# Matmuls that read the un-normalized stream, and interleaved MLP groups, in a two-layer decoder step

## The chip, the cores and the metric

The kernel runs on one core of one Trainium2 chip. The metric is the device time of one execution in microseconds (us).

## What is computed

One inference step of a decoder with two layers over 256 prompt tokens and 8 x 8 sample tokens, 320 tokens in all, each a row of 1024 float32 numbers. Layer 0 mixes with an mLSTM (a matrix memory), layer 1 with block-sparse attention over a paged cache of 64 pages; each layer has an MLP of width 4096 behind it. Around them stands a residual with a LayerNorm after it:

```python
def layer_norm(x, g, b):
    mu = x.mean(-1, keepdims=True)
    var = jnp.square(x - mu).mean(-1, keepdims=True)
    return (x - mu) * lax.rsqrt(var + LN_EPS) * g + b
...
for layer in range(DEPTH):
    h = mlstm_mixer(...) if layer < N_A_LAYERS else attend(q, ctx) @ w_out_b
    x = layer_norm(ALPHA * x + h, ln_g[layer, 0], ln_b[layer, 0])
    x = layer_norm(ALPHA * x + jnp.square(relu(x @ w_up)) @ w_down, ln_g[layer, 1], ln_b[layer, 1])
```

Between the layers `kv = x @ w_kv` gives the keys and values of the second layer, and `q = x @ w_q` its queries. There are four norms: l = 0 behind the mLSTM, 1 behind its MLP, 2 behind the attention, 3 behind the last MLP.

## The kernel before

**Layout.** The stream X lies turned: 128 partitions of model width by 8 chunks by 320 tokens. So a norm's mean is a sum over partitions and chunks, and its mean, variance and rstd are tiles of 128 x 320 with equal rows.

**Dense tiles.** All weights together are 24 quads of 8 tiles, 192 tiles. A tile is 1024 inputs by 128 outputs. Precision is bought with two rounded float32r halves: `split` in ScalarE rounds a weight tile to its high half (L893), `split` in VectorE subtracts for the low half (L1215), and `dense` (L454) multiplies, chunk by chunk, high by high, high by low, low by high: 24 matmuls of 320 columns. There are four buffers of each half, and four of raw weights, each of two tiles, which SyncE loads as they come free. The result of tile t goes to bank t % 2; the tile after next waits until it is read (`evac` counts that). `dense3` (L469) runs three tiles side by side behind a norm, in more banks, chunk by chunk as the norm's chunks come.

**Order.** The quads are the mLSTM's q/k, v and output gate, its output projection Q_WOA, eight for MLP 0, keys, values, queries (Q_WK, Q_WV, Q_WQ), the attention's output projection Q_WOB and eight for MLP 1. Each engine's program is written out in its own order, with semaphores between them. In an MLP a loop of four rounds runs one up quad (1024 of the 4096 hidden units) and its down quad. Of an up tile ScalarE reads the bank with relu (L1037), VectorE squares (L1449), ScalarE rounds to `HH` (L1040), VectorE subtracts to `HL` (L1451). Of a down tile VectorE adds the bank to X (`residual`, L1363 and L1365).

**A norm.** GpSimd sums x and x squared over chunks 0 to 6 (`sums`, L1641 to L1648), TensorE sums over partitions with a matrix of ones (`ln_stats`, L652 to L657), VectorE forms mean and variance (L1399 to L1403), ScalarE takes logarithm and exponential for a first rstd (L1003, L1004), VectorE centres chunks 0 to 3 (L1406) and GpSimd chunks 4 to 7 (L1655), VectorE refines rstd by a Newton step (L1409 to L1411), then multiplies by rstd and applies gain and bias (L1424, L1434, L1419; ScalarE L1012 for some chunks). Only then come the two halves `XH` and `XL` for the next matmuls (L1008, L1018, L1428, L1415). GpSimd afterwards multiplies X by ALPHA (L1662) for the next residual.

**Around the first norm.** During Q_WOA VectorE also updates the sample state (L1386), and GpSimd has prepared the masked values (L1674) while the last output-gate tiles ran. Behind norm 0 `prompt_state` (L636) runs on TensorE, and ScalarE copies and stores its results (L1046 to L1053).

Of the kernel before, what the change touches and what calls it, by code (L numbers as in the profile page):

```python
# [38 lines left out]
SIDE_BY_SIDE = (Q_MLP0, Q_WK, Q_MLP1)  # L39
UPS = [Q_MLP0 + 2 * g for g in range(4)] + [Q_MLP1 + 2 * g for g in range(4)]  # L40
ACT_QUADS = sorted([Q_QK, Q_V, Q_O, Q_WK, Q_WV, Q_WQ] + UPS)
NT = 8 * N_QUADS
RAW, SPL = 4, 4
# [73 lines left out]
def evac(t):  # L117

    q = t // 8
    mine = q in ACT_QUADS  # L120
    before = sum(1 for x in range(q) if (x in ACT_QUADS) == mine)
    return (0 if mine else 1), 8 * before + t % 8 + 1


def build(nc, x_prompt, x_sample, state_C, state_n, state_m, cache_k, cache_v, page_table,
# [4 lines left out]
    with ctx:  # L130
# [21 lines left out]
        HH = put("h_hi", [128, NC8, T], F32R)  # L152
        HL = put("h_lo", [128, NC8, T], F32R)
# [12 lines left out]
        lnT = put("ln_cols", [128, 64])  # L166
        bg = put("b_gate", [40, 1])
# [25 lines left out]
        npr_at = [a[0]]  # L193
# [3 lines left out]
        vm_at, az_at, cq_at = [xh_at], [hh_at], [fs_at]  # L197
# [28 lines left out]
        ln_at = [vreg]  # L226
        mu = put("ln_mu", [128, T], F32, ln_at)
        var = put("ln_var", [128, T], F32, ln_at)
        rs = put("ln_rstd", [128, T], F32, ln_at)
        tmp = put("ln_tmp", [128, T], F32, ln_at)  # L230
        assert ln_at[0] <= b_[0]
# [10 lines left out]
        ko_at, yo_at = [b_[0] - 8192], [b_[0] - 16384]  # L242
# [14 lines left out]
        def sem(name):  # L257
# [4 lines left out]
        s_ev = [sem("act_emptied"), sem("dve_emptied")]  # L262
        s_x = sem("x_in")
# [46 lines left out]
        def dense_bank(t):  # L310


            if t % 8 == 4 and t // 8 in (Q_MLP0, Q_MLP1):
                return ps[5]
            return ps[9 - t % 8] if t % 8 in (2, 3) and t // 8 in SIDE_BY_SIDE else ps[t % 2]

# [19 lines left out]
        def wsrc(u):  # L336

            q, j = u // 4, u % 4
            c = 256 * j
            w, c0 = {Q_QK: (win, 0), Q_V: (win, 1024), Q_O: (win, 2048), Q_WOA: (w_out_a[0], 0),  # L340
                     Q_WK: (w_kv, 0), Q_WV: (w_kv, 1024), Q_WQ: (w_q_b[0], 0), Q_WOB: (w_out_b[0], 0)}[q]
            return lhs_k(w[:, c0 + c:c0 + c + 256])
# [11 lines left out]
        def _(sp):  # L354
            def load_unit(u, src, more=0):
                if isinstance(more, int) and u < RAW:
                    pass
                else:
                    sp.wait_ge(s_lo, 2 * (u - RAW) + 2 + 2 * more)
                sp.dma_start(raw[u % RAW][:, :, :], src).then_inc(s_raw[u % RAW], 16)  # L360
# [5 lines left out]
            load_unit(0, wsrc(0))  # L366
            load_unit(1, wsrc(1))
# [5 lines left out]
            load_unit(2, wsrc(2))  # L373
            load_unit(3, wsrc(3))
# [8 lines left out]
            for u in range(4, 16):  # L383
                load_unit(u, wsrc(u))

            def mlp_loads(first, m):
                with sp.Fori(0, 4) as g:
                    for j in range(4):
                        load_unit(4 * first + j, lhs_k(w_up[m][:, bass.ds(g * 1024 + 256 * j, 256)]), 8 * g)
                    for j in range(4):  # L390
                        load_unit(4 * first + 4 + j,
                                  lhs_k(w_down[m][bass.ds(g * 1024, 1024), 256 * j:256 * j + 256]), 8 * g)

# [1329 lines left out]
```

## Time and profile before

| | us |
|---|---|
| median of 3 runs | 1020.72 |
| lowest, highest | 1020.37, 1023.13 |
| span of the profiled execution | 1020.9 |
| TensorE busy in it | 950.1 |
| VectorE | 566.2 |
| ScalarE | 402.2 |
| GpSimd | 130.4 |
| TensorE, its mean granted clock | 0.964 |

The profile is one execution. Busy shares are averages over stages, so the place to look is the timeline around each norm and the windows of TensorE, not the total. In the rows further down PE is TensorE, PEld its weight loads, DVE VectorE, ACT ScalarE, POOL GpSimd, SPq or ACTq the DMA issues of SyncE or ScalarE; brackets give the idle time before an instruction and who ended it. The granted clock is 1.00 at 2.4 GHz and 0.50 at 1.2 GHz.

### The profile page before, as it was taken

Reading aid. Unit: us, or ns where it says so; the run is one execution under the profiler, and the core shown is the slowest. Engines: PE = TensorE matmul, PEld = TensorE weight load, DVE = VectorE, ACT = ScalarE, POOL = GpSimd, SP = SyncE. Lnnn points to the kernel's source line nnn. Section 1 sums busy time; section 2 is a strip of 40 time slices with the busy share of each in tenths; the row PEclk is TensorE's granted clock in tenths of the full one; section 3 lists DMA queues with packets and bytes.
Section 4 is the critical chain, followed back from the end, with each engine's and each line's share of the span. In section 5 each row is a group of like instructions: output and inputs, shape, how many; then the busy total and the mean of one; then the engine's idle time right before and its main releaser. Section 6 shows DMA issues by size and latency. Waiting matters only on the chain.

```text
span 1020.9 us, 19665 instructions
## 1 busy us (share of the span) xinstructions
PE 950.1 (93%) x7610; PEld 875.7 (86%) x7610; DVE 566.2 (55%) x883; ACT 402.2 (39%) x705; POOL 130.4 (13%) x135
## 2 busy tenths in 40 slices
PE   6999998979999999969999999998788999999994
PEld 5998887869999999959998767775678999999993
DVE  6543677777465555565443475650357656465545
ACT  4423332245353434335434435360244434352423
POOL 0000004641000000362000000000172000000062
PEclk9999999999999999989999999998797999999996
DMA  9932112418444453534637999899831644535301
GB/s 273 266 124 83 42 42 83 106 31 263 151 163 149 141 164 124 165 116 149 233 124 260 397 368 345 291 409 407 303 124 49 199 132 158 165 123 165 123 0 51
DMA packets 130486, 180.16 MB, mean 176 GB/s; under 512 B 5659, under 2 KB 112603, under 8 KB 130420
## 3 DMA queue, kind: packets, MB, share of 16 engines
q1 hardware_dynamic: 125642, 173.96, 50.7%
q10 hardware_dynamic: 4138, 3.17, 1.0%
q0 software_dynamic: 640, 2.10, 0.8%
q8 instruction: 48, 0.79, 0.3%
q14 instruction: 18, 0.15, 0.0%
HBM read 172.90 MB, written 6.31 MB: 176 GB/s over the span
## 4 chain that ended last, share of the span: by engine, by line
PE 82%; DVE 9%; DMA 3%; ACT 2%; issue 2%; SPq 1%; POOL 1%; ACTq 0%; DVEq 0%; POOLq 0%
PE ps L464 21%; PE ps L466 20%; PE ps L465 20%; PE ps L753 5%; PE ps L782 3%; DMA page<-in_cache_v_dram 2%; DVE x L1406 1%; PE ps L831 1%; PE ps L481 1%; PE ps L592 1%; PE ps L485 1%; PE ps L482 1%; DVE ln_tmp L1409 1%; DMA v_tok<-in_x_sample_dram 1%; PE ps L577 1%
## 5 line engine op out<-in xcount | busy, mean ns | idle before, releaser
L1215 DVE TENSOR_TENSOR w_lo<-raw,w_hi 128x1024 fp32r<-128x1024 f32 x192 | 239.8, 1251 | 93.7 <-ACT w_hi L893 93.6
L464 PE MATMUL ps<-x_hi,w_hi 128*128 128x320 f32 x888 | 280.2, 316 | 2.2 <-DVE w_lo L1215 1.1
L893 ACT ACTIVATE w_hi<-raw 128x1024 fp32r<-128x1024 f32 x192 | 202.3, 1054 | 189.9 <-PE ps L466 189.9
L465 PE MATMUL ps<-x_lo,w_hi 128*128 128x320 f32 x888 | 276.9, 312 | 0.0
L466 PE MATMUL ps<-x_hi,w_lo 128*128 128x320 f32 x888 | 276.8, 312 | 0.0
L464 PE MATMUL ps<-h_hi,w_hi 128*128 128x320 f32 x576 | 179.3, 311 | 3.3 <-DVE h_lo L1342 3.3
L465 PE MATMUL ps<-h_lo,w_hi 128*128 128x320 f32 x576 | 178.5, 310 | 0.0
L466 PE MATMUL ps<-h_hi,w_lo 128*128 128x320 f32 x576 | 178.5, 310 | 0.0
L464 PEld LDWEIGHTS ps<-x_hi,w_hi 128*128 128x128 f32 x888 | 169.1, 190 | 3.9 <-issue 1.6
L465 PEld LDWEIGHTS ps<-x_lo,w_hi 128*128 128x128 f32 x888 | 169.3, 191 | 0.0
L466 PEld LDWEIGHTS ps<-x_hi,w_lo 128*128 128x128 f32 x888 | 169.1, 190 | 0.0
L464 PEld LDWEIGHTS ps<-h_hi,w_hi 128*128 128x128 f32 x576 | 108.7, 189 | 7.0 <-DVE h_lo L1342 3.6
L465 PEld LDWEIGHTS ps<-h_lo,w_hi 128*128 128x128 f32 x576 | 108.7, 189 | 0.0
L466 PEld LDWEIGHTS ps<-h_hi,w_lo 128*128 128x128 f32 x576 | 108.6, 189 | 0.0
L1641 POOL COPY sum_x<-x 128x320 f32<-128x320 f32 x4 | 1.8, 455 | 650.1 <-DVE x L1363 646.6
L1363 DVE TENSOR_TENSOR x<-x,ps 128x320 f32<-128x320 f32 x72 | 35.1, 488 | 82.4 <-PE ps L466 81.4
L1037 ACT ACTIVATE fm<-ps 128x320 f32<-128x320 f32 x64 | 27.9, 435 | 101.7 <-PE ps L466 92.1
L753 PEld LDWEIGHTS ps<-base,page 128*128 128x128 f32 x512 | 55.3, 140 | 14.2 <-issue 14.1
L1509 DVE COPY k_turned<-ps 128x512 f32<-128x512 f32 x64 | 43.9, 690 | 40.1 <-PE ps L753 40.0
L753 PE MATMUL ps<-base,page 128*128 128x128 f32 x512 | 62.8, 276 | 1.4 <-DVE k_turned L1509 1.3
L1451 DVE TENSOR_TENSOR h_lo<-sq,h_hi 128x320 fp32r<-128x320 f32 x64 | 31.5, 492 | 48.6 <-ACT h_hi L1040 48.6
L1132 ACT ACTIVATE k_turned<-ps 128x512 f32<-128x512 f32 x64 | 38.2, 597 | 50.2 <-PE ps L753 50.2
(299 smaller groups left out, 1043.0 us busy)
## 6 DMA issues: line engine op xcount, KB each, us to landing
raw<-in_w_up_dram SPq DMA_DIRECT2D x32, 1024.0 KB, 5.4
raw<-in_w_down_dram SPq DMA_DIRECT2D x32, 1024.0 KB, 5.2
page<-in_cache_k_dram SPq DMA_DIRECT2D x64, 512.0 KB, 5.5
page<-in_cache_v_dram SPq DMA_DIRECT2D x64, 512.0 KB, 6.6
raw<-in_w_in_a_dram SPq DMA_DIRECT2D x12, 1024.0 KB, 9.9
raw<-in_w_kv_dram SPq DMA_DIRECT2D x8, 1024.0 KB, 5.6
raw<-in_w_out_a_dram SPq DMA_DIRECT2D x4, 1024.0 KB, 5.2
raw<-in_w_q_b_dram SPq DMA_DIRECT2D x4, 1024.0 KB, 5.9
```

Of the source, the lines that this page charges most:

```text
L464: mm(out, WH[t % SPL][:, k, :], hi[:, k, :], start=(k == 0), stop=False)
L465: mm(out, WH[t % SPL][:, k, :], lo[:, k, :], start=False, stop=False)
L466: last = mm(out, WL[t % SPL][:, k, :], hi[:, k, :], start=False, stop=(k == 7))
L753: last = nc.tensor.transpose(ps[page_banks(P)[h // 4]][:, 128 * (h % 4):128 * (h % 4) + 128], page[P % RING][:, 128 * h:128 * h + 128], ident)
L782: last = mm(ps[SCORE_BANK[2 * a_ + r // 2]][32 * j:32 * j + 32, 256 * (r % 2):256 * (r % 2) + 256], QZ[G][:, 4 * a_ + j, bb, :], KT[pair % ...
L893: A(WH[t % SPL][:, :, :], raw[u % RAW][:, :, 128 * (t % 2):128 * (t % 2) + 128], ACT.Copy)\
L1037: A(FR[n % 2][:, :], o, ACT.Relu).then_inc(s_ev[0], 1)
L1132: A(KT[P // 2 % 2][:, 0:4, 128 * (P % 2):128 * (P % 2) + 128], ps[page_banks(P)[0]][:, :].rearrange("p (h t) -> p h t", h=4), ACT.Copy).th ...
L1215: V.tensor_tensor(WL[t % SPL][:, :, :], raw[(t // 2) % RAW][:, :, 128 * (t % 2):128 * (t % 2) + 128], WH[t % SPL][:, :, :].bitcast(F32), A ...
L1363: ins = V.tensor_tensor(X[:, n, :], X[:, n, :], ps[t % 2][:, 0:T], ALU.add)
L1451: V.tensor_tensor(HL[:, n, :], FS[n % 2][:, :], HH[:, n, :].bitcast(F32), ALU.subtract)\
L1509: V.tensor_copy(KT[P // 2 % 2][:, 4:8, 128 * (P % 2):128 * (P % 2) + 128], ps[page_banks(P)[1]][:, :].rearrange("p (h t) -> p h t", h=4)). ...
```

## The change

The matmuls behind norms 0, 1 and 2 read x times gain, which does not need mean or variance. With W the weights, x' = (x - mu) rs g + b gives

x' W = rs ( (x g) W - mu (g W) ) + b W.

So the moving tile gets two more columns, the gain and the bias (`TW` = 322), and each output tile brings its own g W and b W along. The up tiles are read as y = (x g) W - mu (g W) + sd (b W), where sd = 1/rs; relu(y) squared is then too large by sd squared, and X is left un-normalized with it: the stream is scaled by rs squared only when the last down quad is added. In K, V and Q tiles rs and b W are applied at reading.

Part by part: (a) `dense3` is gone; `first_dense` is one tile of 322 columns, chunk by chunk as `XL` comes, with `ln_stats` behind it. (b) rounding (`x_rounded` on ScalarE, `x_low` on VectorE) follows each residual chunk of the quad before. (c) VectorE evacuates an up tile in two operations; ScalarE then does relu in place and two squares. (d) centring and scaling of X moves wholly to GpSimd (`centred`), gain and bias for the residual to ScalarE (`gained`) and VectorE, in the second up quad. (e) the MLP quads run up 0, up 1, down 0, up 2, down 1, up 3, down 2, down 3, with two pairs of `HH`/`HL`, and are written out instead of looped; dense tiles from MLP 0 on use four banks. (f) K, V, Q are 24 tiles in a row, read in three VectorE steps and one of ScalarE; turning them lags by four tiles. (g) `Vm`, the masked values, lie elsewhere and GpSimd starts them after all heads are gated. (h) prompt state moves behind the second tile, its stores into the first up quad. (i) weight splits run up to five tiles ahead. (j) the first page loads wait for the last MLP 0 tile instead of the scaled stream.

```diff
+MLP_ORDER = [("u", 0), ("u", 1), ("d", 0), ("u", 2), ("d", 1), ("u", 3), ("d", 2), ("d", 3)]
+TW = T + 2
...
-        XH = put("x_hi", [128, NC8, T], F32R)
-        XL = put("x_lo", [128, NC8, T], F32R)
+        XH = put("x_hi", [128, NC8, TW], F32R)
+        XL = put("x_lo", [128, NC8, TW], F32R)
...
         def dense_bank(t):
+            return ps[t % 2] if t // 8 < Q_MLP0 else ps[(0, 1, 6, 7)[t % 4]]
...
+            def first_dense(t, l):
+
+                pe.wait_ge(s_gb, l + 1)
+                if l == 0:
+                    pe.wait_ge(s_cadd, 6)
+                dense(t, XH, XL, lambda k: (s_xl, (8, 16, 32)[l] + k + 1), TW)
+                ln_stats(l)
...
+            def mlp(l, q0, hl0):
+                for i, (kind, g) in enumerate(MLP_ORDER):
                     for n in range(8):
+                        t = 8 * (q0 + i) + n
+                        if i == 0 and n == 0:
+                            first_dense(t, l)
+                        elif kind == "u":
+                            dense(t, XH, XL, None, TW)
+                        else:
+                            if n == 0:
+                                pe.wait_ge(s_hl, hl0 + 8 * g + 8)
+                            dense(t, HH[g % 2], HL[g % 2])
+                        if l == 0 and i == 0 and n == 1:
+                            prompt_state()
...
+            def x_rounded(l, n):
+
+                act.wait_ge(s_xr, 8 * l + n + 1)
+                A(XH[:, n, 0:T], X[:, n, :], ACT.Copy, scale=lnT[:, 8 * l + n:8 * l + n + 1]).then_inc(s_xh, 1)
...
+                        if kind == "u":
+                            split_to(t + (4 if i == 0 and n == 0 else 5))
+                            if i == 0 and n == 0:
+                                rstd(l)
+                            if l == 0 and i == 1 and n == 0:
+                                act.wait_ge(s_co, 16 * 8)
+                            act.wait_ge(s_ev[1], evac(t)[1])
+                            f = FR[n % 2]
+                            own(A(f[:, :], f[:, :], ACT.Relu))
+                            if 8 * g + n >= 2:
+                                act.wait_ge(s_hl, hl0 + 8 * g + n - 1)
+                            A(FS[n % 2][:, :], f[:, :], ACT.Square)
+                            A(HH[g % 2][:, n, :], f[:, :], ACT.Square).then_inc(s_hh, 1)
+                            if i == 1:
+                                gained(l, n)
+                            if l == 0 and i == 0 and n == 4:
+                                prompt_state_out()
...
+            def x_low(l, n):
+
+                dve.wait_ge(s_xh, (8, 16, 32)[l] + n + 1)
+                V.scalar_tensor_tensor(XL[:, n, 0:T], X[:, n, :], lnT[:, 8 * l + n:8 * l + n + 1],
+                                       XH[:, n, 0:T].bitcast(F32), ALU.mult, ALU.subtract).then_inc(s_xl, 1)
...
+                            if i == 0 and n == 0:
+                                split_to(t + 4)
+                                stats(l)
+                                refined(l)
+                                own(V.tensor_tensor(sd[:, :], var[:, :], rs[:, :], ALU.mult))
+                                V.tensor_tensor(rs2[:, :], rs[:, :], rs[:, :], ALU.mult).then_inc(s_lnf, 1)
+                            dve.wait_ge(s_mm, t + 1)
+                            own(V.scalar_tensor_tensor(f[:, :], nmu[:, :], bank[:, T:T + 1], bank[:, 0:T],
+                                                       ALU.mult, ALU.add))
+                            V.scalar_tensor_tensor(f[:, :], sd[:, :], bank[:, T + 1:TW], f[:, :], ALU.mult, ALU.add)\
+                                .then_inc(s_ev[1], 1)
+                            split_to(t + 5)
+                            dve.wait_ge(s_hh, c0 + 8 * g + n + 1)
+                            V.tensor_tensor(HL[g % 2][:, n, :], sq[:, :], HH[g % 2][:, n, :].bitcast(F32),
+                                            ALU.subtract).then_inc(s_hl, 1)
+                            if i == 1:
+                                dve.wait_ge(s_xn, 8 * l + n + 1)
+                                own(V.scalar_tensor_tensor(X[:, n, :], var[:, :],
+                                                           lnA[:, 32 + 8 * l + n:33 + 8 * l + n], X[:, n, :],
+                                                           ALU.mult, ALU.add))
...
+                            V.tensor_tensor(X[:, n, :], X[:, n, :], bank[:, 0:T], ALU.add).then_inc(s_ev[1], 1)
+                            if i == 7:
+                                dve.wait_ge(s_ev[1], evac(t)[1])
+                                V.tensor_tensor(X[:, n, :], X[:, n, :], rs2[:, :], ALU.mult).then_inc(s_xr, 1)
...
+            def kvq(i):
+
+                t = 8 * Q_WK + i
+                u, bank = UK[i % 2], dense_bank(t)
+                dve.wait_ge(s_mm, t + 1)
+                if i >= 2:
+                    dve.wait_ge(s_ev[0], evac(t - 2)[1])
+                V.tensor_scalar(cb[:, t % 4:t % 4 + 1], bank[:, T + 1:TW], QSCALE if i >= 16 else 1.0, None, ALU.mult)
+                own(V.scalar_tensor_tensor(u[:, :], nmu[:, :], bank[:, T:T + 1], bank[:, 0:T], ALU.mult, ALU.add))
+                V.tensor_tensor(u[:, :], u[:, :], rs[:, :], ALU.mult).then_inc(s_uk, 1)
...
             def centred(l):
 
-                pool.wait_ge(s_var, l + 1)
-                for m in range(2, 4):
+                pool.wait_ge(s_lnf, l + 1)
+                pool.wait_ge(s_xl, (8, 16, 32)[l] + 8)
                 for m in range(4):
                     pair = X[:, 2 * m:2 * m + 2, :]
+                    own(G.tensor_tensor(pair, pair, bcast(nmu[:, :], 1, 2), ALU.add))
+                    G.tensor_tensor(pair, pair, bcast((rs if l == 1 else sd)[:, :], 1, 2), ALU.mult)\
+                        .then_inc(s_pc, 1)
...
-            pool.wait_ge(s_mm, 8 * Q_O + 8)
+            pool.wait_ge(s_hg, H)
             pool.wait_ge(s_vc, 8)
```

## Rows read from the trace of the kernel before

**Rows 1.** The page, busy time, its share of the span, instructions.

```profile
PE 950.1 (93%) x7610; PEld 875.7 (86%) x7610; DVE 566.2 (55%) x883; ACT 402.2 (39%) x705; POOL 130.4 (13%) x135
```

**Rows 2.** Timeline of TensorE: start us, us, engine, line, operation; last tiles' last matmuls.

```profile
203.45 0.31 PE L466 MATMUL ps<-h_hi,w_lo 128*128 128x320 f32 x1
...
445.60 0.31 PE L466 MATMUL ps<-h_hi,w_lo 128*128 128x320 f32 x1
...
758.21 0.31 PE L466 MATMUL ps<-x_hi,w_lo 128*128 128x320 f32 x1
...
998.39 0.31 PE L466 MATMUL ps<-h_hi,w_lo 128*128 128x320 f32 x1
```

**Rows 3.** Windows, TensorE: stretch, us, busy (matmuls), granted clock, DMA share, GB/s.

```profile
207.65:212.45 4.80, 4.78 (x39) 1.00 0.00 0
...
300.00:442.00 142.00, 142.00 (x970) 1.00 0.48 154
...
445.75:457.90 12.15, 2.58 (x10) 0.76 0.02 6
...
457.90:462.00 4.10, 4.10 (x15) 0.50 0.00 0
...
758.35:770.50 12.15, 2.58 (x10) 0.82 0.01 3
...
770.50:776.00 5.50, 5.49 (x20) 0.50 0.00 0
```

**Rows 4.** Timeline of the first norm, all engines; idle before and releaser in brackets.

```profile
205.30 0.81 PE L652 MATMUL ps<-sum_x,base 128*128 128x320 f32 x2 [1.54 <-POOL xx L1648]
...
209.04 2.89 DVE L1406 TENSOR_TENSOR x<-x,ln_mu 128x640 f32<-128x640 f32 x2
...
209.21 4.12 POOL L1655 TENSOR_TENSOR x<-x,ln_mu 128x640 f32<-128x640 f32 x2 [3.96 <-DVE ln_var L1403]
...
211.97 1.70 DVE L1409 SCALAR_TENSOR_TENSOR ln_tmp<-ln_rstd,ln_var 128x320 f32<-128x320 f32 x1
...
214.23 0.49 DVE L1411 SCALAR_TENSOR_TENSOR ln_rstd<-ln_tmp,ln_rstd 128x320 f32<-128x320 f32 x1
```

**Rows 5.** Groups by line and shape, whole span: busy us, mean ns | idle before.

```profile
L1215 DVE TENSOR_TENSOR w_lo<-raw,w_hi 128x1024 fp32r<-128x1024 f32 x192 | 239.8, 1251 | 93.7 <-ACT w_hi L893 93.6
...
L893 ACT ACTIVATE w_hi<-raw 128x1024 fp32r<-128x1024 f32 x192 | 202.3, 1054 | 189.9 <-PE ps L466 189.9
...
L1451 DVE TENSOR_TENSOR h_lo<-sq,h_hi 128x320 fp32r<-128x320 f32 x64 | 31.5, 492 | 48.6 <-ACT h_hi L1040 48.6
...
L1040 ACT ACTIVATE h_hi<-sq 128x320 fp32r<-128x320 f32 x64 | 29.7, 464 | 9.2 <-DVE sq L1449 9.2
...
L1365 DVE SCALAR_TENSOR_TENSOR x<-x,ps 128x320 f32<-128x320 f32 x8 | 3.9, 483 | 6.9 <-PE ps L466 6.9
...
L1012 ACT ACTIVATE x<-x,ln_cols 128x320 f32<-128x320 f32 x13 | 8.5, 652 | 15.8 <-DVE x L1419 15.8
```

**Rows 6.** Timeline and a window (TensorE) at the end of the mLSTM heads.

```profile
160.47 9.74 POOL L1674 TENSOR_TENSOR v_masked<-v_tok,base 64x512 f32<-64x512 f32 x8 [105.42 <-PE ps L466]
...
164.76 1.32 DVE L1328 TENSOR_TENSOR sum_xx<-sum_xx,exp_neg_m 128x320 f32<-128x320 f32 x1
...
171.12 0.41 PE L464 MATMUL ps<-h_hi,w_hi 128*128 128x320 f32 x1 [3.35 <-DVE h_lo L1342]
...
173.00:175.00 2.00, 2.00 (x9) 0.50 0.22 48
```

**Rows 7.** Timeline of VectorE, output projection of the first layer.

```profile
192.43 2.15 DVE L1386 SCALAR_TENSOR_TENSOR C<-C,ae_pairs,ps 128x128 f32<-128x128 f32 x8
```

**Rows 8.** Timeline of ScalarE's queue, behind the first norm.

```profile
226.88 1.47 ACTq L1050 DMA_DIRECT2D out_dram<-c_prompt  x2
228.38 1.81 ACTq L1052 DMA_DIRECT2D out_dram<-n_prompt  x1
```

**Rows 9.** Timeline of TensorE, first matmuls behind the query projection.

```profile
551.51 0.65 PE L764 MATMUL ps<-k_attn,q_attn 128*32 128x64 f32 x32 [0.53 <-ACT q_attn L1111]
```

More of the change, by code:

```diff
@@ L119, in evac @@
     q = t // 8
+    if q in SUM_QUADS:
+        return 2, 8 * (0, 2)[SUM_QUADS.index(q)] + t % 8 + 1
     mine = q in ACT_QUADS
-    before = sum(1 for x in range(q) if (x in ACT_QUADS) == mine)
+    before = sum(1 for x in range(q) if (x in ACT_QUADS) == mine and x not in SUM_QUADS)
     return (0 if mine else 1), 8 * before + t % 8 + 1
@@ L382, in _ @@
                                  state_C[0, :, 2 * j + h2].rearrange("b k v -> k b v")).then_inc(s_c0, 16)
[L383 to L392, printed above, removed]
-            mlp_loads(Q_MLP0, 0)
-            for u in range(4 * Q_WK, 4 * Q_WK + 4):
-                load_unit(u, wsrc(u))
+            for u in range(4, 4 * Q_WK + 4):
+                load_unit(u)
             sp.wait_ge(s_co, 16 * 8)
@@ L452, in _, with dense @@
             mm = nc.tensor.matmul
[L454 to L460 removed]
+            def dense(t, hi, lo, chunk_ready=None, width=T):
+                before = 2 if t < 8 * Q_MLP0 + 2 else 4
+                if t - before >= 0:
+                    pe.wait_ge(*emptied(t - before))
+                pe.wait_ge(s_lo, t + 1)
+                out = dense_bank(t)[:, 0:width]
                 for k in range(8):
@@ L1459, in _ @@
-            ln(0)
-            dve.wait_ge(s_np, 1)
-            own(V.tensor_tensor(nout[:, :].rearrange("p (h k) -> p h k", h=8),
-                                n0[:, :].rearrange("p (h k) -> p h k", h=8), bcast(cols[0:8, 48:56], 2, DK), ALU.mult))
-            V.tensor_tensor(nout[:, :], nout[:, :], ps[6][0:8, :], ALU.add).then_inc(s_nadd, 1)
-            with dve.Fori(0, 4) as g:
-                mlp_round(Q_MLP0, g, 8)
-            ln(1)
-            for n in range(8):
-                split(8 * Q_WK + n + 3)
@@ L1692, in _ @@
             for n in range(7):
-                sums(2, Q_WOB, n)
+                sums(2, n)
             centred(2)
-            scaled(2)
             for n in range(7):
-                sums(3, N_QUADS - 1, n)
-            centred(3)
+                sums(3, n)
+            pool.wait_ge(s_var, 4)
+            for m in range(2, 4):
+                pair = X[:, 2 * m:2 * m + 2, :]
+                G.tensor_tensor(pair, pair, bcast(nmu[:, :], 1, 2), ALU.add).then_inc(s_pc, 1)
 INS = ["x_prompt", "x_sample", "state_C", "state_n", "state_m", "cache_k", "cache_v", "page_table", "w_in_a",
```

546 lines of the change are left out of this document (261 added, 285 removed).

## Prediction

> **What bounds the kernel now.** I read the busy times first: TensorE works in 950.1 of 1020.9 us [rows 1], so the question is what its remaining 71 us are and how much of its busy time runs at half clock. Next the timeline of TensorE alone. A dense tile is 24 float32r matmuls of 320 columns. In the MLP it does nothing else: 970 matmuls in 142.00 us, 142.00 us busy [rows 3], 146.6 ns from start to start, 3.52 us a tile. So the other engines are hidden there, and 64 MLP tiles are worth 225.3 us at this pace.
>
> Then the places where that pace breaks. The last matmuls of the four stretches that end in a norm start at 203.45, 445.60, 758.21 and 998.39 us [rows 2]. From the first to the second lie 242.15 us. Tiles take 225.3, the sums of the norm on TensorE 2.35 (from their start at 205.30 [rows 4] to 207.65, where the next products start) and those products, of the prompt state, 4.8 [rows 3]; 9.7 us are lost. From the third to the fourth lie 240.2 us, less 225.3 and 2.35: 12.5 lost. Behind the second norm I add up what is lost: 12.15 us with 2.58 busy is 9.6 idle, and then 15 matmuls take 4.10 us at a granted clock of 0.50 where 2.2 would do, 1.9 more: 11.5 [rows 3]. The three norms inside cost 33.7 us. The wait is a serial chain [rows 4]: the column sums, mean and variance, the logarithm and exponential on ScalarE, centring (two multiplications by rows of 640 on VectorE beside two on GpSimd), the refinement, gain, rounding. After each idle stretch of 12.15 us TensorE comes back at half clock (1.2 of its two levels 1.2 and 2.4 GHz), for 4.1 and 5.5 us [rows 3].
>
> **What the change removes.** The matmul behind the norm gets x times gain before mean and deviation are known, so its chunks are ready as the residual chunks are. Chunk 7 is the last: after the last tile of the stretch come the residual 0.48, one low-half split 1.25 (queued ahead of it), the low half of x 0.49 and two handovers, about 2.4 us; ScalarE's split 1.05 and rounding 0.46 run beside it [rows 5]. TensorE reaches chunk 7 after 21 matmuls, 3.1 us. So the first tile does not stop, the sums follow it, and all 33.7 us are free to go. Idle gaps gone, half clock goes too; it is inside the 33.7.
>
> A second edit lies earlier. The masked values (L1674) no longer wait for the last output-gate tile, but for all gated heads. Now GpSimd's 9.74 us of it run from 160.47 [rows 6], beside the chain of the last head: its operation at 164.76 takes 1.32 us, where 0.49 is the usual time of that size [rows 5], so 0.8 is lost; the low half before it and the product behind it lose 0.8 and 0.7, the split 0.6. TensorE meanwhile waits 3.35 us until 171.12 and then runs at 0.50 of its clock (9 matmuls in 2.00 us) for about 3.4 us [rows 6]. Moved, the chain ends 2.8 us earlier; the last low half now meets GpSimd, so 0.8 comes back. The gap falls to about 1.4 us, and gaps of 1.5 us (before 205.30 [rows 4]) were not followed by half clock. Gain: 2.0 and 1.5, together 3.5. The first state product, at 177.8, finds its masked values by 173.
>
> Sum of gains: 37.2 us.
>
> **What it adds.** (1) Two columns (gain, bias) on 64 up tiles and 24 K/V/Q tiles: 88 x 24 = 2112 matmuls of 322 columns. In proportion, 2/320 of 146.6 ns is 0.9 ns each: 1.8 us. No row has a matmul of another width in float32r; bounds are 0 (if something other than columns paces it) and 13 us (6 ns each, as if the pace of 146.6 ns, 13.3 more than 320 columns at 2.4 GHz, were caused by start addresses and grew by half of that with the rows of x now 1288 bytes apart). I take 1.8, as the half-clock pace of 267 ns is exactly its columns. The Trainium skill (TensorE: Matmul & The Clock Gate, Back-to-back issue gap) gives columns over 2.4 plus 2.5 ns: 135.8 ns for 320 columns; the trace has 146.6, so the page does not price this stream, though by it the two columns would cost the same 1.8 us.
>
> (2) The up tiles' own chain. VectorE now evacuates with two operations of 0.49 (0.48 for the nearest row, scalar_tensor_tensor from a bank) [rows 5], then a split 1.25, then the low half 0.49; ScalarE does a split 1.05, relu, and square twice, 0.46 each [rows 5]. If VectorE is never late both fit into 3.54. If it is late, the loop is evacuation 1.05, three ScalarE operations 1.4, low half 0.5 and handovers: 3.05 us a tile, so it catches up 0.5 a tile. In the second up group each tile also has the residual's gain on ScalarE (0.65, L1012 [rows 5]) and its bias on VectorE (0.5): the late loop is 3.7, losing up to 0.17 x 8 = 1.4 us of a lead it may not have.
>
> (3) The start of each stretch. The statistics need 8.7 us from the sums to both factors (from 205.30 to the end of the refinement, L1411, at 214.7 it is 9.4; without L1406 in front, and with 0.49 for L1409, it is 7.7; two new products are 1.0) [rows 4]. On the clock of the first norm: last tile ends 203.6, first tile 207.1, sums 209.3, factors 216. TensorE may run three more tiles into three free banks; the fifth tile needs the first bank at 219.9. But from 216 on GpSimd centres and scales x, 8 operations over 640 elements, while VectorE works. What one costs the other is in [rows 4]: VectorE's second L1406 and its L1409 (1.70, else 0.49) end only after GpSimd's current operation; one such GpSimd operation alone is 1.4 us. VectorE's second evacuation, split and low half have both inputs in SBUF and wait 0.7 on average, 1.4 when back to back. Followed tile by tile: evacuations at 218.3, 225.6, 230.2, 233.7, wanted at 219.9, 223.4, 229.2, 233.8. Stalls 2.2 + 1.0 = 3.2 us in the last MLP. In the first one the prompt-state products (4.8 us, now behind the second tile) cover most of it: 0.6. There, though, ScalarE issues the prompt-state stores in the middle of the up group: DMA issues 1.47 and 1.81 [rows 8] and two copies, 4.4 us in which the next splits and squares wait; TensorE is then 2.7 late. In the stretch before, the low half of x (0.49 to 1.0) comes on top of state additions 2.15 [rows 7], a split and a residual in a step of 4.7 us (a tile and the state products), and makes chunk 7 about 1.1 late. With (2), first MLP 0.6 + 2.7 + 1.1 + 1.4 = 5.8, last MLP 3.2 + 1.4 = 4.6. K/V/Q: the loop per tile is shorter, 1.5. Bounds for each stretch: 0 and 9.
>
> (4) Tails. The query tile is evacuated in three VectorE steps and one on ScalarE before the attention may start, where one ScalarE copy and 0.53 us of waiting stand now [rows 9]: 1.1 us more. The last MLP group multiplies by 1/variance per chunk, which lies in front of the last norm's sums: 0.55, and up to 0.9 for GpSimd: 1.0.
>
> Costs: 1.8 + 5.8 + 4.6 + 1.5 + 1.1 + 1.0 = 15.8. At no cost: the interleaved group order (a down group starts a whole group after its inputs, loads are the same megabytes in another order, DMA share 0.48 in the MLP [rows 3]); the loops written out; the page loads' new release (they still queue behind the V weights). The stage of the pages is paced by its own transfers and ring, and moves as a whole.
>
> 37.2 - 15.8 = 21.4; 1020.9 - 21.4 = **999.5 us**. The profiled span is within 0.2 us of the median 1020.72, so nothing is added for what lies around it.
>
> **Rivals.** *A, all covered.* VectorE meets GpSimd less than I count, and ScalarE's issues are absorbed. Left are 1.8, 1.1 and 0.6: 1020.9 - 37.2 + 3.5 = 987. For it: the MLP shows no idle TensorE at all now. Against: the 12 us gap that gave everybody time to catch up is gone.
>
> *B, the port.* VectorE waits for every centring operation in full: 8 x 1.4 = 11.2 us a norm against the 6 or so I let it lose, and each later tile inherits it: some 4 us more at three norms, 1011.5. For it: L1409 waited nearly a whole operation. The Trainium skill says this as a rule (SBUF — State Buffer, Who interferes with whom): the pair of ports shared by VectorE and GpSimd is locked for a whole instruction, and a VectorE operation with two SBUF inputs needs it. The trace agrees: 1.70 against 0.49.
>
> *C, slower: the up tile's chain becomes the bound.* Nothing in the trace shows an operation that takes its per-partition scalar from a bank, and there are two per up tile, on the path from bank to free bank. At 0.49 the late loop is 3.05. It decides from 3.87 us a tile: (3.87 - 3.54) x 64 = 21.4. At 4.0 us, that is 0.48 more on each of the two, the loss is 29 us: 1029. Against: the nearest row, 0.48, already reads the bank and an SBUF operand.
>
> *D, it doesn't do what it says:* something at the end of the stretch (the low half of x behind the split, or the sums) still holds the first tile, so that TensorE idles as before: 1018 to 1021.
>
> **How the numbers follow.** Forecast (994 to 1006) 0.50; A and what lies towards it (986 to 994) 0.20; B and stalls of that size (1006 to 1017) 0.15; D, or C in part, within 0.3% (3 us, about what a measurement can tell from no change) 0.07; C 0.08. Faster 0.85, same 0.07, slower 0.08. The range for 8 in 10 is 987 to 1012: the forecast, most of A and B.
>
> **What would show it.** Right: behind each inner norm matmuls at 147 ns without a gap of 12 us and a granted clock of 1.00 there; the norm's sums between the first and second tile; short waits at the fifth to seventh tile of each MLP, released by VectorE; GpSimd's centring beside stretched VectorE operations; half clock at 173 us gone. Wrong: an up group slower than 3.6 us a tile throughout (C), matmuls of 322 columns over 149 ns (the columns), or the attention stage longer than before.

## The result, and the profile after

The changed kernel takes 1041.07 us (median of 4 runs, 1037.98 to 1042.78) against 1021.76 for the kernel before on the same chip: a ratio of 1.0187, 95% interval 1.0164 to 1.021. It is slower by about 19 us, where 999.5 was forecast; the range did not hold it. The profiled execution has a span of 1040.8 us.

The page of the changed kernel, TensorE's busy time and the shares of the chain that ended last:

```profile
PE 962.4 (92%) x7610; PEld 886.6 (85%) x7610; DVE 650.1 (62%) x1033; ACT 447.8 (43%) x796; POOL 160.5 (15%) x141
PE 77%; DVE 12%; ACT 4%; issue 3%; SPq 2%; DMA 1%; POOL 0%; DVEq 0%; ACTq 0%; POOLq 0%
```

TensorE is busy 12 us longer than in [rows 1], although it has hardly more to compute: that is half clock or overlapping ends, and the windows must say where. I cut both timelines at the first matmul of each stage. The times are us; the forecast column sorts the terms of the prediction by the same cuts. The 1.8 for two columns go in as 0.65 for each MLP and 0.5 for K/V/Q, and of the 9.7, 11.5 and 12.5 us lost at the inner norms 4.0, 1.9 and 2.7 lie behind the cut, in the next stage. Besides, the change carries work across the cuts at no gain: the sums of each inner norm (2.35) and the products of the prompt state (4.8) ran ahead of the next stage's first tile, and now run behind it.

```
stage                                     before    after   change   forecast
start to W_O of layer A, and W_O + norm   216.49   200.17   -16.3     -15.2
first MLP + norm                          241.41   234.56    -6.9      -3.5
K/V/Q and the pages                       270.68   318.01   +47.3      +3.5
W_O of layer B + norm                      41.93    30.14   -11.8     -12.1
last MLP + last norm                      250.39   257.92    +7.5      +5.9
sum                                      1020.90  1040.80   +19.9     -21.4
```

Four stages came out within 3.4 us of the forecast (together -27.5 against -24.9). One stage lost 47.3 instead of 3.5. Inside it the loop over K, V and Q has 23 tiles from its first matmul to the first of the last tile: 457.90 to 547.30 us before (89.4), 434.73 to 565.20 after (130.5), so 41.1 us are lost in the loop. The other 6.3 lie behind it, with the pages.

Windows of TensorE in the changed kernel (stretch, us, busy and count for each engine, granted clock, DMA share, GB/s): the MLP, then the loop from its start at 434.73.

```profile
205.00:417.00 212.00, 211.85 (x1435) 207.99 (x1434) 150.31 (x204) 107.96 (x171) 23.00 (x18) 1.00 0.49 155
434.73:449.00 14.27, 13.57 (x86) 12.67 (x85) 10.21 (x18) 6.55 (x8) 5.03 (x5) 1.00 0.33 112
449.00:464.00 15.00, 14.81 (x99) 14.26 (x99) 13.31 (x13) 5.48 (x7) 14.45 (x8) 1.00 0.26 78
464.00:472.89 8.89, 5.73 (x33) 5.45 (x32) 6.67 (x13) 4.48 (x10) 0.00 (x0) 0.81 1.01 361
485.00:554.00 69.00, 46.73 (x239) 44.67 (x239) 23.34 (x48) 17.20 (x29) 1.84 (x2) 0.80 0.21 67
```

Behind the second norm, where [rows 3] had 2.58 us of work in 12.15 and then a clock of 0.50, the first of the K/V/Q rows has 13.57 busy in 14.27 at 1.00: the norm is gone, as forecast. But from 485 to 554 us TensorE is busy 46.7 of 69 us at a clock of 0.80, and the DMA engines are nearly idle (0.21), so it is not a transfer. The waits of TensorE in the changed kernel from 434 to 570 us (line, releaser, us in total, times, longest):

```profile
PE ps L490 <- DVE v_tok L1324: 18.3, 6, 3.1
PE ps L490 <- ACT turned L1077: 7.1, 3, 3.2
PE ps L475 <- DVE x_lo L1401: 0.7, 1, 0.7
```

L490 is the first transpose of a turn of a K or V tile (`kv_turn`). It waits for the bank of the turn before last, which VectorE's `v_copy` (L1323, L1324) or ScalarE's `kv_out` (L1076, L1077) has to empty. One of the six waits, from the timeline of the changed kernel (TensorE's last matmul of a tile, then all engines):

```profile
511.81 0.31 PE L477 MATMUL ps<-x_hi,w_lo 128*128 128x322 f32 x1
512.22 1.06 ACT L883 ACTIVATE w_hi<-raw 128x1024 fp32r<-128x1024 f32 x1 [8.26 <-PE ps L477]
513.30 1.23 DVE L1238 TENSOR_TENSOR w_lo<-raw,w_hi 128x1024 fp32r<-128x1024 f32 x1 [6.96 <-ACT w_hi L883]
514.45 0.42 DVE L1323 COPY v_tok<-ps 128x256 f32<-128x256 f32 x1
514.78 0.27 DVE L1324 COPY v_tok<-ps 64x128 f32<-64x128 f32 x1
515.20 0.45 PE L490 MATMUL ps<-base,sq 128*128 128x128 f32 x1 [3.08 <-DVE v_tok L1324]
```

Read it from the bottom. The turn at 515.20 waited for the copy at 514.78. That copy had had its data for long, but stood in VectorE's program behind the low half of a weight split; the low half waited for ScalarE's high half (8.26 us idle before it), and that for the buffer which the tile ending at 512.1 had just set free. In the code: at step i VectorE does `kvq(i)`, `split_to(t + 5)` and then `v_copy(i - 12)`. The split of tile t+5 needs the matmuls of tile t+1, since four weight buffers are in the ring. TensorE, right behind the matmuls of tile t+1, makes turn i-2 (turns 8 to 15 are those of V) and for that needs `v_copy(i - 12)`. So split, low half and copy, 1.06 + 1.23 + 0.7, lie bare between two tiles. Each time it costs 3 us in which TensorE has nothing to do.

Two points of the change come together here. In the kernel before, the V copy stands behind a split as well (VectorE, `split(8 * Q_WV + n + 3)` and then `v_copy(n - 1)`), but that is the split of tile t+3, and its buffer has been free since the matmuls of tile t-1. The changed kernel splits two tiles further ahead, as (i) in the list of the change says. And (f) says that the turns lag by four tiles: the code does that for the K tiles alone, while turns 8 to 15 are `kv_turn(i - 3)`.

My theory A: this order costs the 41 us, by six waits of 3 us and the half clock that they bring. Rivals: the backlog from GpSimd's centring beside VectorE (B), transfers (C).

### The profile page after: what moved, and what is told of

Same layout as the page of the kernel before. It is cut to its first block, busy times and chain, and to the rows that moved or that the text cites. A ratio compares the mean times of both kernels' runs of the same rounds, so it can differ in the third digit from the quotient of the medians.

```text
span 1040.8 us, 19155 instructions
## 1 busy us (share of the span) xinstructions
PE 962.4 (92%) x7610; PEld 886.6 (85%) x7610; DVE 650.1 (62%) x1033; ACT 447.8 (43%) x796; POOL 160.5 (15%) x141
## 4 chain that ended last, share of the span: by engine, by line
PE 77%; DVE 12%; ACT 4%; issue 3%; SPq 2%; DMA 1%; POOL 0%; DVEq 0%; ACTq 0%; POOLq 0%
PE ps L475 20%; PE ps L477 19%; PE ps L476 19%; PE ps L742 5%; DVE w_lo L1238 3%; PE ps L771 3%; ACT w_hi L883 2%; PE ps L820 1%; SPq L414 1%; SPq L418 1%; PE ps L591 1%; DVE fm L1476 1%; DMA page<-in_cache_v_dram 1%; DVE h_lo L1480 1%; DVE x_lo L1401 1%
## 5 line engine op out<-in xcount | busy, mean ns | idle before, releaser
L475 PE MATMUL ps<-x_hi,w_hi 128*128 128x322 f32 (+1 forms) x896 | 289.2, 323 | 5.6 <-DVE fm L1476 4.8
L476 PE MATMUL ps<-x_lo,w_hi 128*128 128x322 f32 (+1 forms) x896 | 283.6, 317 | 0.0
L477 PE MATMUL ps<-x_hi,w_lo 128*128 128x322 f32 (+1 forms) x896 | 283.5, 316 | 0.0
L475 PE MATMUL ps<-h_hi,w_hi 128*128 128x320 f32 x640 | 199.0, 311 | 2.2 <-DVE h_lo L1371 1.1
L477 PE MATMUL ps<-h_hi,w_lo 128*128 128x320 f32 x640 | 198.0, 309 | 0.0
L476 PE MATMUL ps<-h_lo,w_hi 128*128 128x320 f32 x640 | 198.0, 309 | 0.0
L475 PEld LDWEIGHTS ps<-h_hi,w_hi 128*128 128x128 f32 x640 | 120.9, 189 | 6.4 <-DVE x L1394 3.4
L477 PEld LDWEIGHTS ps<-h_hi,w_lo 128*128 128x128 f32 x640 | 120.8, 189 | 0.0
L820 PE MATMUL ps<-page,probs_turned 128*32 128x128 f32 x1024 | 40.4, 303 | 9.0 <-DMA page<-in_cache_v_dram 7.5
L1036 ACT ACTIVATE fm<-fm 128x320 f32<-128x320 f32 x64 | 29.6, 463 | 43.9 <-DVE fm L1476 43.9
```

The lines of the kernel that those rows point to most:

```text
L475: mm(out, WH[t % SPL][:, k, :], hi[:, k, 0:width], start=(k == 0), stop=False)
L476: mm(out, WH[t % SPL][:, k, :], lo[:, k, 0:width], start=False, stop=False)
L477: last = mm(out, WL[t % SPL][:, k, :], hi[:, k, 0:width], start=False, stop=(k == 7))
L820: last = mm(o_bank(G, bb)[32 * j:32 * j + 32, c:c + 128], PT[G][:, 8 * a_ + p, 32 * j:32 * j + 32], page[g % RING][:, 128 * h:128 * h + 12 ...
L1036: own(A(f[:, :], f[:, :], ACT.Relu))
```

## Experiments

**The copy ahead of the split.** VectorE's order in the loop, and nothing else:

```
                 kvq(i)
-                split_to(min(t + 5, 8 * Q_WOB + 3))
                 if 12 <= i < 20:
                     dve.wait_ge(s_tp, i - 3)
                     v_copy(i - 12, s_tv, ps[4 + i % 2])
+                split_to(min(t + 5, 8 * Q_WOB + 3))
```

> In the K/V/Q loop on VectorE the copy of the turned V tile is put ahead of the weight split of the same step; nothing else changes. Theory A (the copy stands behind a split that needs the next tile's matmuls, so each V turn on TensorE waits some 3.0 us, six times, and the clock falls to half between): the six waits of 3.0 us go (18) and with them most of the half clock (six tiles of 8.1 to 9.8 us become about 3.6 to 4.0, less the waits some 12): 1041 - 30 = 1011 us, range 1005 to 1018. The two or three turns that wait for ScalarE's copy of a turned K tile keep their 2 us each. Theory B (the stage is late because VectorE is slowed beside GpSimd's centring, and the backlog never clears): the waits move to another releaser and the time stays within 5 us of 1041. Theory C (the stage is paced by transfers, Q weights beside the page prefetch): unchanged, 1041.

Measured: 1014.18 us, 0.9927 of the kernel before (0.9902 to 0.9952). The waits of TensorE from 434 to 535 us in this kernel:

```profile
PE ps L490 <- ACT turned L1077: 7.1, 3, 3.2
PE ps L490 <- DVE v_tok L1324: 0.4, 2, 0.2
```

The six waits for the V copy, 18.3 us, are down to 0.4, and the three for ScalarE stand as they were, 7.1. The loop takes 102.9 us instead of 130.5: 27.6 less, 18 of waiting and 9 to 10 that the half clock had added. That is theory A; B and C said that the time would stay within 5 us of 1041.

**The turn a tile later.** The same distance given back on TensorE instead:

```
-                if 4 <= i < 12:
-                    kv_turn(i - 4)
-                if 11 <= i < 19:
-                    kv_turn(i - 3)
+                if 4 <= i < 20:
+                    kv_turn(i - 4)
```

> Instead of the order on VectorE, TensorE's turns of V move one tile later (turn i-4 after tile i for all 16 turns; before, from tile 11 on, turn i-3); nothing else changes. Theory A: the V turns find their bank free, and so do the two turns at tiles 11 and 12 that waited for ScalarE's copy of K: 1041 - 30 - 5 = about 1005 us, range 999 to 1012, and the K/V/Q stage up to the start of the W_O product of layer B falls from 318 to some 280 us. Theory B: within 5 us of 1041. Theory C: 1041. If this gains like v_copy_first or more, it is the distance of one tile that costs, whichever side gives it back.

Measured: 1006.96 us, ratio 0.9847 (0.9808 to 0.9886). The loop takes 95.9 us, all V tiles 3.90, and of the waits for ScalarE one of 3.2 us is left. Windows of this kernel over V and Q, and the first K tiles:

```profile
474.00:530.00 56.00, 56.00 (x389) 55.86 (x388) 37.33 (x76) 28.40 (x49) 1.85 (x2) 1.00 0.51 162
434.37:467.80 33.43, 29.31 (x188) 27.59 (x186) 27.60 (x38) 14.54 (x20) 19.53 (x12) 0.99 0.39 123
```

TensorE is never idle from 474 to 530 us and its clock is 1.00, where the kernel after had 0.80. This edit stands alone, not on top of the first. It gains 7.0 us more in the loop, since the two turns at tiles V.3 and V.4 had the same fault with `kv_out`: they stood a tile too early for ScalarE as well. Their two waits, 1.8 and 2.2 us, are gone. One loose end is left in the K tiles, 29.3 busy in 33.4.

**One early turn.** On top of the later turns and of the edit of the tail (below), turn 12 alone goes back to the early place:

```
-                if 4 <= i < 20:
+                if 4 <= i < 20 and i != 16:
                     kv_turn(i - 4)
+                if i == 15:
+                    kv_turn(12)
```

> v_turn_later_tail with one of the sixteen turns (number 12) made a tile earlier, as the kernel after has it for eight. Theory A: this one turn waits for a V copy that stands behind a split which needs the tile just finished: one wait of some 3.0 us ahead of it and nothing else, so that tile V.7 takes 3.9 + 0.35 + 3.0 = about 7.2 us, at full clock or with a short stretch of half clock (then up to 10). The other V tiles stay at 3.90. Rival (the early turns cost only as a row, by keeping VectorE and ScalarE behind): under 1 us.

It ran once, in 1009.18 us, 2.5 above the median of its base (1006.69); single runs of the base lie some 5 us apart, so its profile has to tell. There tile V.7 takes 7.11 us instead of 3.90, the next one 5.16 instead of 3.90, all other V tiles stay. From its timeline, and two of its windows:

```profile
504.99 1.23 DVE L1238 TENSOR_TENSOR w_lo<-raw,w_hi 128x1024 fp32r<-128x1024 f32 x1 [1.03 <-ACT w_hi L883]
506.47 0.27 DVE L1324 COPY v_tok<-ps 64x128 f32<-64x128 f32 x1
506.89 0.30 PE L490 MATMUL ps<-base,fm 128*128 128x128 f32 x1 [2.69 <-DVE v_tok L1324]
496.00:500.00 4.00, 4.00 (x30) 3.99 (x29) 2.77 (x6) 1.51 (x2) 0.00 (x0) 1.00 0.12 28
507.20:510.00 2.80, 2.80 (x15) 2.80 (x14) 0.56 (x2) 0.00 (x0) 0.00 (x0) 0.62 0.92 290
```

The clock is 1.00 before the wait of 2.69 us and 0.62 behind it. So one such turn costs 3.2 us of waiting and 1.3 of half clock, with the cause put in by hand. It works as a dose: one gives 4.5, six gave 27.6, or 4.6 each.

**No centring.** The rest of the loop's loss (K.4 to K.7 at 4.15, 4.30, 7.52 and 5.04 us) and the stalls of the last MLP point at GpSimd. On top of the later turns, its eight centring operations per norm are left out:

```
-                    own(G.tensor_tensor(pair, pair, bcast(nmu[:, :], 1, 2), ALU.add))
-                    G.tensor_tensor(pair, pair, bcast((rs if l == 1 else sd)[:, :], 1, 2), ALU.mult)\
-                        .then_inc(s_pc, 1)
+                    G.memset(SQ[:, m + 1:m + 2], 0.0).then_inc(s_pc, 1)
+                pool.wait_ge(s_pc, 4 * l + 4)
```

> v_turn_later, and GpSimd's eight centring operations of each of the three inner norms are left out (the stream then lacks the subtraction and the scaling by the deviation, so later values are those of another stream; the work of the other engines is the same). Theory P (VectorE and GpSimd slow each other, VectorE's split 1.3 -> 2.6 us beside them): the tiles beside them fall to 3.55 us: in the last MLP 6.1+6.0+5.2-10.7 = 6.7 us, in the K tiles 4.1+4.3-7.1 = 1.3 and part of the 7.5 us tile, in the first MLP 0.5 to 1: 8 to 14 us below v_turn_later. Rival (the stalls of tiles 4 to 6 come from VectorE's own chain of norm arithmetic at the start, not from GpSimd): 0 to 2 us below.

Measured: 996.17 us, ratio 0.9745 (0.9713 to 0.9777), 10.8 us below `v_turn_later`. Windows of this kernel, the K tiles and the first up group of the last MLP:

```profile
434.97:467.80 32.83, 32.13 (x214) 31.19 (x213) 23.25 (x42) 16.65 (x25) 4.02 (x8) 1.00 0.58 193
743.19:773.78 30.59, 30.59 (x203) 29.96 (x202) 23.12 (x36) 18.66 (x29) 2.48 (x7) 1.00 0.48 140
```

and the same two of `v_turn_later`:

```profile
434.37:472.74 38.37, 34.25 (x215) 32.51 (x213) 30.24 (x42) 16.52 (x25) 19.53 (x12) 0.96 0.47 155
748.30:784.12 35.82, 32.57 (x202) 31.41 (x201) 28.64 (x33) 17.71 (x29) 17.18 (x11) 0.95 0.40 117
```

The eight K tiles fall from 38.4 to 32.8 us, the eight up tiles from 35.8 to 30.6. VectorE is busy 7.0 and 5.5 us less (42 operations in both K rows, 33 and 36 in the up rows). The price of GpSimd beside VectorE is therefore 5.5 us in the K tiles, 5.2 in the last MLP and under 1 in the first (tile 5, 3.90 against 3.55, and its neighbours). The rival, that VectorE's own norm arithmetic makes the stalls, expected at most 2.

Which operations suffer is in the trace of the changed kernel: one line at a time, in a stretch beside the centring (449 to 464, 795 to 812 us), then in one without it (474 to 490, 815 to 900). Columns are line, engine, operation, count, ns min/median/max.

```profile
L1517 DVE SCALAR_TENSOR_TENSOR kvq<-ln_neg_mu,ps x3: 536/536/537, 453.8 to 462.3; 128x320 f32<-128x320 f32 x3
L1517 DVE SCALAR_TENSOR_TENSOR kvq<-ln_neg_mu,ps x4: 544/544/545, 475.2 to 486.9; 128x320 f32<-128x320 f32 x4
L1518 DVE TENSOR_TENSOR kvq<-kvq,ln_rstd x4: 1215/1220/1448, 448.3 to 462.9; 128x320 f32<-128x320 f32 x4
L1518 DVE TENSOR_TENSOR kvq<-kvq,ln_rstd x4: 492/492/493, 475.7 to 487.5; 128x320 f32<-128x320 f32 x4
L1238 DVE TENSOR_TENSOR w_lo<-raw,w_hi x3: 2472/2575/2575, 451.3 to 459.8; 128x1024 fp32r<-128x1024 f32 x3
L1238 DVE TENSOR_TENSOR w_lo<-raw,w_hi x5: 1224/1226/1226, 473.9 to 489.5; 128x1024 fp32r<-128x1024 f32 x5
L1476 DVE SCALAR_TENSOR_TENSOR fm<-ln_std,ps,fm x3: 1240/1241/1515, 796.2 to 810.1; 128x320 f32<-128x320 f32 x3
L1476 DVE SCALAR_TENSOR_TENSOR fm<-ln_std,ps,fm x17: 556/556/557, 816.7 to 898.1; 128x320 f32<-128x320 f32 x17
L1480 DVE TENSOR_TENSOR h_lo<-sq,h_hi x2: 1854/1856/1857, 801.7 to 807.7; 128x320 fp32r<-128x320 f32 x2
L1480 DVE TENSOR_TENSOR h_lo<-sq,h_hi x17: 491/493/493, 815.7 to 897.1; 128x320 fp32r<-128x320 f32 x17
```

The first evacuation, one operand in SBUF and one in a bank, keeps its 0.54 us. Those with both tensors in SBUF go from 0.49 to 1.22 or 1.86 and from 1.23 to 2.58. The Trainium skill (SBUF — State Buffer, Who interferes with whom) draws the line just there: outside VectorE's two-port modes, an instruction with at most one SBUF input does not contend with GpSimd, and one with two does. The trace agrees, 0.54 against 1.22 and more.

**Centring spaced.** The work is needed, but not at once. GpSimd also waits for a tile's matmuls before each operation, in the K/V/Q stage only; `v_turn_later_tail` is the base:

```
+                    if l == 1:
+                        pool.wait_ge(s_mm, 8 * (Q_MLP0, Q_WK, Q_MLP1)[l] + 5 + 2 * m)
                     own(G.tensor_tensor(pair, pair, bcast(nmu[:, :], 1, 2), ALU.add))
+                    if l == 1:
+                        pool.wait_ge(s_mm, 8 * (Q_MLP0, Q_WK, Q_MLP1)[l] + 6 + 2 * m)
```

> v_turn_later_tail, and in the K/V/Q stage alone GpSimd's eight centring operations are let go one per tile (tiles 4 to 11) instead of back to back. Theory P (VectorE's step in a K tile is 2.4 us alone and 4.28 us beside unbroken GpSimd work, so the backlog reaches TensorE in tiles K.4 to K.7): one GpSimd operation per tile adds about 1.2 us, 3.6 us fits into a tile of 3.55 + 0.35 us with its turn, and the four tiles of 4.1, 4.3, 7.5 and 5.1 us fall to about 3.9: 5 us below v_turn_later_tail, at 997 to 1001 us by the profile. Rival (it is the amount of GpSimd work, not its density, that costs): 0 to 1 us below.

Measured: 1001.14 us, ratio 0.9803 (0.9782 to 0.9824). K.4 to K.7 take 3.80, 3.89, 3.89 and 3.90, and the loop 90.4 us, as without any centring, against 96.0 in its base. For the K tiles it is the density that costs, not the amount: VectorE has slack there. The tile times show this; the ratio alone, 0.9803 against 0.9832 for the base, is 3 us with intervals that overlap.

The same in the MLPs (without the two conditions):

> k_centring_spaced, and the centring in the two MLPs one operation per tile too (tiles 4 to 11). There VectorE's step is 3.0 us of 3.55 alone in the first up group and 3.6 in the second. Theory P in numbers: 1.2 us more per tile does not fit (4.2 in tiles 4 to 7, 4.8 in 8 to 11, against 3.55), so the backlog only moves to later tiles: the last MLP's excess of 5.2 us stays within 2 us of that, perhaps grows to 7. Rival (density is what costs): the excess falls under 1 us and the kernel gains 4 to 5 us more.

Measured: 1000.61 us, ratio 0.9787 (0.9771 to 0.9803). In the last MLP tiles 4 to 6 (6.14, 6.05, 3.69 us) fall to 3.55, 3.55 and 3.82, and then five tiles of 3.98 and one of 4.57 follow: an excess of about 3.9 instead of 5.2. In the first MLP, where the products of the prompt state had covered the bunched operations, a tile of 5.37 appears. So in the up tiles VectorE has too little slack (0.55 + 0.56 + 1.22 + 0.49 = 2.8 of 3.55 us are its own) and the cost moves, as theory P said, if by less.

Spaced in the K tiles and the last MLP, bunched in the first (`if l >= 1`):

> v_turn_later_tail with the centring let go one operation per tile in the K/V/Q stage and in the last MLP, back to back in the first MLP. From the tile times of the runs so far: 1.8 us (a tile of 5.37 instead of 3.6 at the start of a group) come back against all_centring_spaced, and against k_centring_spaced the last MLP keeps its gain of 5.2 - 3.9 = 1.3 us. So 999 us, range 997 to 1001. Rival (the two variants differ by nothing that adds up): 1000.6 to 1001.1, as both.

Measured: 999.70 us, ratio 0.9791 (0.9765 to 0.9817). Its tiles are as computed, but the intervals of the three spaced kernels overlap: which of them is best is not settled. All three are faster than both kernels given.

**The tail.** On ScalarE and VectorE the split of W_O's fourth weight tile needs the last Q tile and stood ahead of the read of the tile before:

```
-                split_to(min(t + 5, 8 * Q_WOB + 3))
+                split_to(min(t + 5, 8 * Q_WOB + (3 if i == 23 else 2)))
```

> v_turn_later, and the split of the last of W_O's first four weight tiles no longer stands ahead of the second to last Q tile's read on ScalarE and VectorE (it needs the last Q tile's matmuls). Theory T (the wait of 4.1 us ahead of the scores is this queueing; the read itself is 0.15+0.54+0.49+0.55 = 1.7 us): 2 to 2.5 us below v_turn_later. Rival (the page stage is paced by its transfers, and what its start gains is given back): 0 to 0.5 us below.

Measured: 1006.69 us, ratio 0.9832 (0.9796 to 0.9869), against 1006.96 without: no difference in the medians. The first matmul of the scores, in the changed kernel and then in this one:

```profile
572.97 1.08 PE L753 MATMUL ps<-k_attn,q_attn 128*32 128x64 f32 x32 [4.06 <-ACT q_attn L1092]
```

```profile
539.45 0.65 PE L751 MATMUL ps<-k_attn,q_attn 128*32 128x64 f32 x32 [2.48 <-ACT q_attn L1090]
```

The wait falls from 4.06 to 2.48 and the time from the last Q tile to W_O from 187.50 (`v_turn_later`) to 184.27 us; but this execution has tiles of 10.78 and 10.35 us among the 9.07 of the output-gate stage, which cost it the same 3. Such tiles stand in that stage in seven of the eleven profiles here (10.70 and 10.45 in the kernel before), and I don't know why. The stretch from the last Q tile to W_O settles the mechanism: it takes 184.3 to 185.9 us in the five profiles with this edit and 187.1 to 187.5 in the four of the changed kernel's order without it, some 2 us less, as theory T had it. The gain isn't in the medians.

**The masked values alone.** The kernel before with the one line of the other edit:

```
-            pool.wait_ge(s_mm, 8 * Q_O + 8)
+            pool.wait_ge(s_hg, H)
```

> The kernel before with one line changed: GpSimd's masked values wait for all gated heads instead of the last output-gate tile. The prediction's number: 3.5 us less, the gap of 3.35 us on TensorE ahead of the first W_O tile shrinks to about 1.4 and the half clock behind it goes: 1017.5 us. Rival (the work only moves: the masked values arrive later and the state products or the low halves wait instead): 0 to 2 us less.

Measured: 1019.67 us, ratio 0.9972 (0.9959 to 0.9985), by the ratio 2.9 us less, 1.5 to 4.2 by its interval. The gap ahead of W_O, in this kernel:

```profile
167.69 0.42 PE L464 MATMUL ps<-h_hi,w_hi 128*128 128x320 f32 x1 [1.12 <-DVE h_lo L1342]
169.00:173.00 4.00, 4.00 (x35) 3.73 (x41) 3.56 (x8) 0.70 (x2) 4.00 (x2) 1.00 0.42 116
```

3.35 us of waiting [rows 6] are 1.12, and the clock behind them is 1.00 instead of 0.50. In the changed kernel the first gap is the same, but a state product then waits for VectorE, which neither this kernel nor the one before has:

```profile
166.68 0.41 PE L475 MATMUL ps<-h_hi,w_hi 128*128 128x320 f32 x1 [1.09 <-DVE h_lo L1371]
173.96 1.09 PE L625 MATMUL ps<-v_masked,wsk 32*32 32x512 f32 x16 [2.16 <-DVE wsk L1415]
```

## Why the prediction was wrong, and where it was right

**The step that failed** is the sentence "K/V/Q: the loop per tile is shorter, 1.5". I had compared how much each engine does per tile, and found all of them below a tile's time. That is true: without the fault the loop runs at 3.90 us a tile in V and at 1.00 clock. What I did not do is to follow the order, and put beside each instruction of the new loop what it waits for and what stands behind it. The same prediction said in its first MLP how issues on ScalarE hold up the splits behind them; for the K/V/Q loop it has no word on the order (`split_to` of tile t+5 ahead of `v_copy`, turn i-3), and the wait of TensorE for a turn's bank was put at nothing without a reason. The loss of the loop, by the runs (first matmul of K to the first of the last Q tile, us; `v_copy_first` and `v_turn_later` are alternatives, each an edit of the changed kernel, and the second also takes away two waits for ScalarE):

```
kernel                       loop    step
before                       89.4
after                       130.5
v_copy_first                102.9   27.6  V copy behind the split: 18 waiting, 9 to 10 half clock
v_turn_later                 95.9    7.0  K copy, the same fault on ScalarE
k_centring_spaced            90.4    5.5  GpSimd bunched beside VectorE
```

40.1 of the 41.1 us are named that way. The last 1.0 is a net sum: the two columns and the norm's sums (2.35), which now lie inside the loop, against the half clock that the kernel before had at its start (1.9), and small differences. In the up groups of the MLPs the code has the evacuation ahead of the split, and without the centring their tiles run at 3.55 us from the fourth on.

**Rival C** ended on the slower side with 1029 us, but not by this mechanism. The up tile is 3.55 us long, not 3.87: the operations with a per-partition factor from a bank take 0.55 and 0.56 us (L1474, L1476), which is 0.06 over my 0.49. It was wrong as a reason even though its sign was right; the forecast gave the slower side 0.08, and no rival looked at the loop that failed.

**The norms: right.** The stages of the three inner norms changed by -16.3, -6.9 and -11.8 us against -15.2, -3.5 and -12.1. Of the first, 1.6 is no work of the change: the long output-gate tiles took 3.1 us extra in the profile before and 1.5 in the one after. The surplus of the second is in the first MLP, not in the norm: its 64 tiles (226.36), the norm's sums and the prompt-state products leave 1.1 us of its 234.56, where the forecast had 5.8 of stalls. The prediction took the 12.15 us of [rows 3] as one idle stretch; the norm's sums lie in it, and the longest single idle time is 8.76 us, up to 457.90. No gap of either length and no half clock is left behind any of them: the granted clock is 1.00 from 434.73 to 449 (above), and in these two rows for the first and the third.

```profile
200.20:205.00 4.80, 4.80 (x30) 4.30 (x30) 4.24 (x5) 2.71 (x4) 4.74 (x6) 1.00 0.81 231
783.00:797.00 14.00, 14.00 (x90) 13.37 (x89) 10.24 (x16) 6.44 (x8) 3.33 (x4) 1.00 0.51 149
```

**The masked values: right in size, not in full in the changed kernel.** 3.5 forecast, 2.9 (1.5 to 4.2) measured alone. In the changed kernel the first two W_O tiles take 12.7 us instead of 14.3, so 1.6 of it comes through; the prediction had looked at the masked values of the first state product, and it waits 2.16 us for another input (`wsk`).

**Two columns: mis-sized.** Eight up tiles take 28.43 us and eight down tiles 28.16 (293.43 to 321.86 to 350.02 us in `v_copy_first`): 1.4 ns a matmul instead of 0.9, 3.0 us in all instead of 1.8.

**The port.** The forecast took 1.4 us for one centring operation of GpSimd alone, a figure that no row shows. In the changed kernel they take 1.5 to 2.6 us, and the eight of a norm 15.0 to 15.8, where rival B had 11.2. The forecast let VectorE lose about 6 us a norm, rival B 11.2. The last MLP stalled 5.2 to 6.7 us where I had 3.2; the first under 1, as said, because the prompt-state products cover it; and in the K tiles I had counted nothing, where it costs 5.5. The 2.7 us for ScalarE's stores in the first MLP did not appear: without the centring all tiles behind the prompt state's products are 3.55 to 3.67 us. The last norm (first matmul of the last group to the end) took 50.5 us before and 50.9 after, and 51.0 to 52.0 in the other kernels of this order: 0.4 to 1.5 against 1.0 forecast.

**"The stage of the pages moves as a whole": nearly.** From the last Q tile to W_O it takes 187.5 instead of 181.3 us: the wait for the query tile is 4.1 us instead of 0.53 [rows 9], where I had 1.1 more, and a clock of 0.93 from 570 to 595 us follows. I had costed the four operations of the read, and again not the split that is queued ahead of them. A longer attention stage was one of the prediction's own signs of being wrong.

With the loop mended (later turns, spaced centring, and the edit of the tail with them), the rest of the sum stands: 999.7 to 1001.1 us, 999.5 forecast. That agreement is partly luck: the first MLP stalled 4.7 us less than I had, and the columns (1.2 more), the port in the last MLP (2.0 more) and the tail took most of that back.

## What to carry to other kernels

When a loop is rewritten, count the order and not only the work: for every instruction in it write down which tile's matmuls it needs, and check that nothing behind it on the same engine is needed by TensorE before its next tile. With a ring of four buffers and splits that run to tile t+5, a split is tied to the tile that has just ended, so small evacuations belong ahead of it, or the turn that needs them belongs a tile further back. And elementwise work given to GpSimd should be let go one operation per tile, in tiles where VectorE has slack: beside it VectorE's operations with one input in a bank kept their time, those with both inputs in SBUF did not.

## What the runs showed of the hardware

One wait of 2.7 us of TensorE was enough for a clock of 0.62 in the 2.8 us behind it, while gaps of 1.1 us were followed by 1.00. The two shorter waits of `v_copy_first` lie closer together: behind 1.79 us (to 490.77) the clock stayed 1.00 for the next 4 us of matmuls, and behind 2.18 us (to 497.05) it was 0.64 for 2.9 us. Repeated waits of 3 us at each tile held it at 0.80 over 69 us, so a wait of 3.0 us cost 4.6. VectorE beside GpSimd: an operation with both inputs in SBUF went from 0.49 to 1.22 or even 1.86 us, one with a bank as an input stayed at 0.54. A matmul of 322 float32r columns costs 1.4 ns more than one of 320.
